# Who issues the fetches of the sums' raw blocks: SyncE between pairs of weight chunks instead of ScalarE's queue

## What is computed

```
def swiglu(xn, w_gate, w_up, w_down):
    return (jax.nn.silu(xn @ w_gate) * (xn @ w_up)) @ w_down
```

## Time and profile before

| | us |
|---|---|
| median of 3 runs (2210.8 to 2216.45) | 2215.08 |
| the profiled execution's own time | 2212.44 |
| its span in the profile | 2210.6 |
| PE busy | 2080.7 (94%) |
| DVE busy | 1437.4 (65%) |
| ACT busy | 1183.7 (54%) |
| POOL busy | 834.6 (38%) |
| mean granted TensorE clock, share of full speed | 0.982 |

### The profile page before, as it was taken

The page is one execution under the profiler, slowest core; times in us unless marked ns, Lnnn a source line. Parts: engine busy times, 40 slices in busy tenths (PEclk is TensorE's granted clock), DMA queues, the critical chain, the costliest instruction groups (busy, mean ns, idle before and its releaser), DMA issues.

```text
span 2210.6 us, 34966 instructions
## 1 busy us (share of the span) xinstructions
PE 2080.7 (94%) x11738; PEld 1815.3 (82%) x11738; DVE 1437.4 (65%) x2525; ACT 1183.7 (54%) x2186; POOL 834.6 (38%) x601
## 2 busy tenths in 40 slices
PE   8999999888899988889999999999999998888998
PEld 6778888788888878888887788888878887888886
DVE  5597854767662377676258789899677347666523
ACT  4575753565652356665244467777655345565522
POOL 2232451644433273433327601211364326444331
PEclk9999999999999999999999999999999999999999
DMA  5323262454533245543325322222444434454331
GB/s 175 114 81 98 82 219 95 148 176 165 176 114 95 83 145 170 172 166 128 96 87 165 123 67 82 73 77 89 159 153 152 153 97 160 160 175 159 124 95 67
DMA packets 101460, 282.80 MB, mean 128 GB/s; under 512 B 9224, under 2 KB 34056, under 8 KB 100848
## 3 DMA queue, kind: packets, MB, share of 16 engines
q1 hardware_dynamic: 51120, 182.08, 26.0%
q10 hardware_dynamic: 45696, 83.90, 11.1%
q0 software_dynamic: 4544, 15.55, 2.2%
HBM read 261.03 MB, written 18.89 MB: 127 GB/s over the span
## 4 chain that ended last, share of the span: by engine, by line
PE 74%; DVE 12%; issue 6%; ACTq 3%; ACT 3%; DMA 2%; DVEq 0%; POOL 0%; SPq 0%
PE bank L189 21%; PE bank L191 20%; PE bank L190 20%; PE bank L196 2%; PE bank L195 2%; DMA w_raw<-stream 2%; DVE s_lo L703 2%; DVE w_lo L163 2%; ACTq L357 1%; PE bank L2231 1%; DVE t_lo L699 1%; DVE h L729 1%; ACTq L355 1%; ACT snaps L575 1%; PE bank L985 1%
## 5 line engine op out<-in xcount | busy, mean ns | idle before, releaser
L163 DVE TENSOR_TENSOR w_lo<-w_raw,w_hi 128x1024 fp32r<-128x1024 f32 (+1 forms) x337 | 419.4, 1259 | 394.5 <-ACT w_hi L158 391.4
L158 ACT ACTIVATE w_hi<-w_raw 128x1024 fp32r<-128x1024 f32 (+1 forms) x337 | 331.8, 987 | 486.3 <-PE bank L191 224.0
L189 PE MATMUL bank<-xn_hi,w_hi 128*128 128x512 f32 (+1 forms) x1192 | 434.1, 364 | 3.4 <-DVE w_lo L163 3.2
L191 PE MATMUL bank<-xn_hi,w_lo 128*128 128x512 f32 (+1 forms) x1192 | 420.1, 352 | 0.0
L190 PE MATMUL bank<-xn_lo,w_hi 128*128 128x512 f32 (+1 forms) x1192 | 419.1, 352 | 0.0
L189 PE MATMUL bank<-t_hi,s_hi 128*128 128x256 f32 x648 | 196.4, 303 | 84.5 <-ACT snaps L575 75.3
L189 PEld LDWEIGHTS bank<-xn_hi,w_hi 128*128 128x128 f32 x1192 | 226.4, 190 | 33.6 <-DVE w_lo L163 4.9
L191 PEld LDWEIGHTS bank<-xn_hi,w_lo 128*128 128x128 f32 x1192 | 225.7, 189 | 31.0
L190 PEld LDWEIGHTS bank<-xn_lo,w_hi 128*128 128x128 f32 x1192 | 226.3, 190 | 28.3 <-issue 2.6
L189 PE MATMUL bank<-down_hi,w_hi 128*128 128x512 f32 x528 | 205.7, 390 | 6.3 <-POOL down_lo L856 6.3
L189 PEld LDWEIGHTS bank<-t_hi,s_hi 128*128 128x128 f32 x648 | 131.4, 203 | 95.0 <-ACT snaps L575 85.2
(11 more groups left out here) (489 smaller groups left out, 4994.5 us busy)
## 6 DMA issues: line engine op xcount, KB each, us to landing
w_raw<-stream SPq DMA_DIRECT2D x337, 512.0 KB, 3.7
s_raw<-stream ACTq DMA_DIRECT2D x54, 512.0 KB, 4.2
s_holes<-stream ACTq DMA_DIRECT2D x48, 512.0 KB, 4.7
spill_g<-gate_out ACTq DMA_DIRECT2D x16, 256.0 KB, 2.0
m_more<-spill_g POOLq DMA_DIRECT2D x3, 1024.0 KB, 10.9
s_first<-stream ACTq DMA_DIRECT2D x6, 512.0 KB, 4.3
x<-xt SPq DMA_DIRECT2D x4, 512.0 KB, 6.5
x<-xt ACTq DMA_DIRECT2D x1, 2048.0 KB, 9.4
```

The source lines that it names most:

```text
L158: nc.scalar.activation(w_hi[:, slot, at], w_raw[:, slot % 2, at], ACT.Copy).then_inc(split_hi, 1)
L163: nc.vector.tensor_tensor(w_lo[:, slot, at], w_raw[:, slot % 2, at], w_hi[:, slot, at], ALU.subtract).then_inc(split_lo, 1)
L189: nc.tensor.matmul(to, a_hi, b_hi, start=start, stop=False, skip_group_check=True)
L191: return nc.tensor.matmul(to, a_lo, b_hi, start=False, stop=stop, skip_group_check=True)
```

## The change

Three edits. ScalarE issues no raw fetch any more (the two single calls, `third_raw` and its calls are taken out; the loop over bodies is written a little differently, with the same calls of `seven`). SP's single loop over pairs of chunks is cut up: each feed-forward hands SP a part (`sp_part`) that runs the pairs of its stream in the same order, and puts a wait and the two raw fetches of a tile between two pairs. `raw_to` and the waits ahead of it are the same conditions on the same semaphores, but for tile (0, 0), where the wait is for GpSimd's last addition of squares, and tile (0, 1), where the wait for GpSimd's four activation sums is now written out.

```diff
+        sp_parts = []
+
+        def next_pair(sp, i):
+
+            for slot in range(2):
+                sp.wait_ge(split_lo, 2 * i + (slot - 1))
+                sp.dma_start(w_raw[:, slot, :], stream[2 * i + slot]).then_inc(loaded[slot], 16)
...
-                raw_to(act, 0, 0)
...
-                def third_raw(i, q):
-                    of, to = {-1: ((i, 0), (i + 1, 0)), 0: ((i, 1), (i + 1, 1)), 1: ((i + 1, 0), (i + 2, 0))}[q]
-                    act.wait_ge(c["lo"], part_made("lo", *of, 4))
-                    raw_to(act, *to)
...
-                    if t == 2:
-                        raw_to(act, 0, 1)
                     silu_of(t % 2, 2 * t + 2 * b + 1)
-                third_raw(0, -1)
                 for q in range(2):
                     seven(0, q, True)
-                    third_raw(0, q)
-                with act.Fori(1, BODIES - 2) as i:
+                with act.Fori(1, BODIES - 1) as i:
                     for q in range(2):
                         seven(i, q, True)
-                        third_raw(i, q)
-                for q in range(2):
-                    seven(BODIES - 2, q, True)
-                    if q == 0:
-                        third_raw(BODIES - 2, q)
                 for q in range(2):
                     seven(BODIES - 1, q, q == 0)
...
+            def sp_part(sp, first_pair):
+                at = first_in // 2 + PLAIN
+                with sp.Fori(first_pair, at) as i:
+                    next_pair(sp, i)
+                sp.wait_ge(m["added"], nb["added"] + KT - 1)
+                raw_to(sp, 0, 0)
+                next_pair(sp, at)
+                sp.wait_ge(c["sum"], c0["sum"] + 4)
+                raw_to(sp, 0, 1)
+                next_pair(sp, at + 1)
+                sp.wait_ge(c["lo"], part_made("lo", 0, 0, 4))
+                raw_to(sp, 1, 0)
+                with sp.Fori(1, BODIES - 1) as i:
+                    next_pair(sp, 2 * i + at)
+                    sp.wait_ge(c["lo"], part_made("lo", i - 1, 1, 4))
+                    raw_to(sp, i, 1)
+                    next_pair(sp, 2 * i + (at + 1))
+                    sp.wait_ge(c["lo"], part_made("lo", i, 0, 4))
+                    raw_to(sp, i + 1, 0)
+                last = BODIES - 1
+                next_pair(sp, 2 * last + at)
+                sp.wait_ge(c["lo"], part_made("lo", last - 1, 1, 4))
+                raw_to(sp, last, 1)
+                next_pair(sp, 2 * last + at + 1)
+                return 2 * BODIES + at
+
+            sp_parts.append(sp_part)
...
-            with sp.Fori(1, CHUNKS // 2) as i:
-                for slot in range(2):
-                    sp.wait_ge(split_lo, 2 * i + (slot - 1))
-                    sp.dma_start(w_raw[:, slot, :], stream[2 * i + slot]).then_inc(loaded[slot], 16)
+            pair = 1
+            for sp_part in sp_parts:
+                pair = sp_part(sp, pair)
+            with sp.Fori(pair, CHUNKS // 2) as i:
+                next_pair(sp, i)
```

## The result

The changed kernel takes 2224.82 us (median of 9 runs, 2220.3 to 2228.45), the kernel before 2216.45 in the same series (9 runs). The ratio is 1.004, with a 95% interval of 1.0027 to 1.0054: slightly slower, where 2134 was forecast and 2112 to 2172 was the range. The profiled execution took 2227.1 us, with a span of 2225.3.

The account below looks back on a forecast made before the run. TensorE was taken as bound by late ScalarE copies behind raw fetches; 75.9 us from 42 tiles at 10.6, plus 1.9 and 3 at the start, gave 80.8 saved: 2131.6, plus 2.6 for the median, 2134 us; range 2112 to 2172.

Parts of the forecast that it names:

- What bounds the kernel: TensorE waits for ScalarE's bank copies, 81.6 us in all, late behind ScalarE's s_lo wait and raw fetch issues.
- the tile without the fetch: Feed-forward tiles with no raw fetch ahead on ScalarE take 10.08 us against 12.41; 42 tiles lose 97.7 us.
- the start: First tiles of each feed-forward: 1.9 us from tile (0, 1)'s gaps, 3 from chunk 11 issued before its raw pair.
- rival 1: Clean: no new wait in the tiles, 10.08 us each, gain 102.6, so 2112 us; chance 0.17.
- The clock: TensorE's clock dips go with the gaps; their 22.6 us are inside the 12.41 a tile, no separate term.
- SyncE's order: On SyncE, chunk pairs wait early in a tile, raw pairs at its end; neither holds up the other: 0 us.
- The cover: Chunks queued behind a late s_lo land after 8.4 us with the raw pair, covered by a tile of 10.08.
- Rival 4: SyncE held up: high parts wait for their chunk instead of the fetch, the gap keeps its size, 2215 us; chance 0.03.
- Rival 2: VectorE and GpSimd obstruct each other in most tiles, 11.0 to 11.9 us each, 2153 to 2191 us; chance 0.12.
- VectorE and GpSimd in each other's way: VectorE operations wait beside GpSimd's sums: 0 to 1.9 us a tile added, 0.5 taken, so 10.6 a tile.
- My two margins of 0.7 us: Spare time before TensorE needs ScalarE's copy, and before it needs VectorE's addition of x: 0.7 us each.
- Rival 3: Only ScalarE's issue time comes back, 14.6 us a feed-forward, 44 in all, so 2171 us; chance 0.05.

Follow-up runs that it names:

- the aligned kernel: The changed kernel with SyncE's order in f2 cut at single chunks, both chunks of a tile ahead of the s_lo wait and raw pair: 2116.75 us.
- the wait kept: Against the aligned kernel, ScalarE still waits for the last s_lo at the old fetch's place, issuing nothing: 2174.28 us.
- the two half changes: Against the kernel before, SyncE fetches raw blocks in f0 and f1 only, or in f2 only, ScalarE elsewhere: 2149.97 and 2288.52 us.
- the pair-later kernel: The changed kernel with each raw pair in f2 issued one pair of chunks later, pairs kept whole: 2131.27 us.

## Why the prediction was wrong

**What bounds the kernel, and the tile without the fetch.** Right. TensorE's 10.08 us a tile is nearly what f0 and f1 came to, 10.17 and 10.21. The excess of 97.7 us for 42 tiles plus the start, 102.6 in rival 1, is close to what the aligned kernel gains: 101.1 us. That kernel, 2116.75, lies in the range of 2112 to 2172; the change as made does not. The clock went with the gaps, as said: 1.00 in f0 and f1.

**SyncE's order.** This is the step that failed. "The chunk pair of a tile waits for the two `low_part` early in a tile, the raw pair for the `s_lo` at its end ... So neither holds up the other in the steady loop, and I take 0." It is true where a pair of chunks is a tile, in f0 and f1. I took `at = first_in // 2 + PLAIN` for the first chunk of the loop without working out `first_in` for each feed-forward. From the stage list, which gives the count of chunks of each stage, f2's is 271. There the up chunk of a tile stands behind both the wait and the raw pair. The cost of the order is 0 for f0 and f1 and about 108 us for f2, of which 74 show against the kernel before.

**The cover.** I held that chunk and raw pair one behind the other, 8.4 us, are covered by a tile of 10.08. The 8.4 is close to the 8.11 measured. But the cover is not a tile. In the example TensorE goes on 1.05 us after the chunk landed (1988.46 to 1989.51), so without a gap of 5.54 it was wanted at 1982.92, 2.6 us after the last `s_lo`. So 4 to 6 of the 8 became a gap, and the half clock behind it made that 7 us a tile. A cover has to be counted from the moment at which the transfer can leave to that at which it is wanted.

**Rival 4** named this mechanism, SyncE held up and high parts waiting for their chunk, with a chance of 0.03 and a time of 2215. The mechanism came, though its second half, twice the traffic on the ring, did not by itself cost anything (the aligned kernel has it too). That its time is near the measured one is chance: 2224.8 is the sum of 61 us gained and 74 lost. I put it in all three feed-forwards at a size that just kept the old gap. Where it occurs it costs more than the old gap (17.14 us a tile against 12.41), and in all three it was 2437.58. Rival 2's times were added up 2 us too high: by its own tiles and the start term they are 2151 to 2189.

**VectorE and GpSimd in each other's way.** Mis-sized. I took 0.5 us a tile; it is about 0.1 (10.17 in f2 of the aligned kernel against 10.08). The longer waits within operations did come. The aligned kernel's L728 and L729, now L726 and L727 (duration ns min/median/max):

```profile
L726 DVE TENSOR_TENSOR silu<-silu,norm_r x54: 691/1150/1812, 437.7 to 1976.8; 128x512 f32<-128x512 f32 x54
...
L727 DVE TENSOR_TENSOR h<-h,norm_r x54: 414/1518/1530, 438.3 to 1977.4; 128x256 f32 x42, 128x256 f32<-128x256 f32 x12
```

Medians of 1.150 and 1.518 us against 0.878 and 0.418, and 0.692 and 0.417 without sums. Yet TensorE hardly waited: in 160 us of f0, f1 and f2 it does 1334, 1321 and 1322 matmuls with the sums, and 1335 in f0 without. My two margins of 0.7 us were enough nearly always. The lock that the Trainium skill describes ("SBUF — State Buffer", section "SBUF: two separate sides") is what these rows agree with: 1.518 us with GpSimd's sums, 0.417 without. It cost time mainly in the plain tiles, where the run without sums gains 20 of its 28 to 30 us.

**Rival 3, only the issue time.** Its 44 us is what the issues are worth by themselves, 40.4 with the wait kept. The Trainium skill's rule for this rival ("DMA: Bandwidth & Descriptors", section "Issuing engines are not separate DMA queues") prices the issue alone. The other 57 us was the wait that stood in front of it, which moved with it. And the run with ScalarE issuing later shows that 86 us come back with no change of the issuing engine.

**The start.** I took 3 us for chunk 11 going ahead of its raw pair. In the aligned kernel its transfers in f0, f1 and f2 are

```profile
425.65 3.67 DMA w_raw<-stream
...
786.01 4.28 DMA w_raw<-stream
...
1794.11 3.59 DMA w_raw<-stream
```

against 4.42, 5.48 and 5.59. From a feed-forward's first high part of x to the S4 block of tile (0, 0), the three add up to 196.2 us before and 193.2 there: the term of 3 came. In the change itself they add up to 195.8, so hardly any of it; f2 has the misplaced pair, and why f1's transfer is as long as before (5.67) is not known. f0's gain of 31.5 us is then nearly all tiles: 14 at 12.36 less 10.17 us, 30.7.

**What stays open.** The 2.7 against 8.4 us between the two half changes and the change itself may be noise. Why only every second up chunk of the pair-later kernel comes too late is not shown; the pairs ahead of these are the ones into the halves of rows, whose issues take longer.

## What to carry to other kernels

When an instruction moves to another in-order queue, write out that queue's order for every instance of the loop, with the numbers, the parity of a chunk index included; one instance in three was off by one chunk and cost more than the other two gained. What an issue costs on an engine includes the wait in front of it, here the larger part, and where that wait goes, everything queued behind it goes too. A wait at the end of a tile may stand ahead only of what is wanted a tile later.

## What the runs showed of the hardware

- A chunk of 512 KB issued right behind two raw transfers of 512 KB on the same queue landed in 6.34 us, and in 3.71 with nothing right ahead of it. Over f2's loop the ranges are 4.7 to 7.1 us and 3.3 to 3.7, so the raw pair ahead of it cost it some 2 us.
- An issue costs its engine by its shape: 0.33 us for a chunk with whole rows, 0.57 and 0.54 for one into the halves of rows (the chain at 1980.53 and 1981.29).
- TensorE's granted clock was 0.80 over 160 us of f2, where it idled 4 to 6 us in each tile; 0.95 to 0.97 with gaps of up to 2.9; 1.00 in the run with the wait kept, whose waits were 2.0 at most, over 160 us of f0; and 1.00 with none. Behind a gap of 4 us it ran at 0.51, the lower of its two levels (1.2 GHz), for 5.3 us. So in f2 a gap of 5 us made a tile 7 longer.
- VectorE can lose 30 us in 160 beside GpSimd's sums (148.44 busy against 118.03) with one matmul lost on TensorE (1334 against 1335, f0); the three loops together lost 9 us.
